# Down projection of the last 64 tokens by fetched table rows, with all up projections first

## The reference, cut to what matters

```python
top_v, top_i = lax.top_k(sc, PEER_TOPK)
...
ids = jnp.take_along_axis(cand_id, best_j, axis=-1)
gates = jax.nn.softmax(best_v, axis=-1)
def block(args):
    xb, ib, gb = args
    ub = jnp.take(u_tab, ib, axis=0)
    a = jnp.einsum('td,ted->te', xb, ub, preferred_element_type=jnp.float32)
    w = gb * jax.nn.gelu(a, approximate=False)
    vb = jnp.take(v_tab, ib, axis=0)
    return jnp.einsum('te,ted->td', w.astype(vb.dtype), vb)
```

## Time and profile before

| | us |
|---|---|
| median of three runs (lowest to highest) | 1292.38 (1290.53 to 1292.54) |
| span of the profiled execution, first to last instruction | 1288.8 |
| PE busy in the span | 1253.4 |
| DVE busy | 980.7 |
| ACT busy | 756.8 |
| POOL busy | 385.8 |

### The profile page before, as it was taken

One profiled execution on the slowest core, in us unless ns is written; L12 is line 12 of the kernel. 1 busy time (PEld: TensorE's weight loads), 2 busy tenths in 40 slices (PEclk: granted clock), 3 DMA queues, 4 the chain that ended last, 5 costly groups with the idle time before them and its releaser, 6 DMA issues.

```text
span 1288.8 us, 26239 instructions
## 1 busy us (share of the span) xinstructions
PE 1253.4 (97%) x8596; PEld 1136.5 (88%) x8596; DVE 980.7 (76%) x1851; ACT 756.8 (59%) x1293; POOL 385.8 (30%) x254
## 2 busy tenths in 40 slices
PE   7999999999999989999999999999999999999997
PEld 7999999898999979999999888888888888888885
DVE  6999988997987767997999765656666666666666
ACT  6434454565766655558999645455555555555554
POOL 1189812225160147788888200000000000000000
PEclk9999999999999999999999999999999999999999
DMA  9978876453776245554443565556665556655662
GB/s 374 336 243 258 263 252 224 162 169 111 246 236 210 92 157 177 168 182 146 129 139 122 163 192 184 193 182 227 210 192 184 184 189 195 183 185 185 195 187 74
DMA packets 69344, 248.15 MB, mean 193 GB/s; under 512 B 7968, under 2 KB 8352, under 8 KB 68512
## 3 DMA queue, kind: packets, MB, share of 16 engines
q1 hardware_dynamic: 59920, 213.04, 51.1%
...
HBM read 244.66 MB, written 2.62 MB: 192 GB/s over the span
## 4 chain that ended last, share of the span: by engine, by line
PE 60%; DVE 8%; ACT 6%; issue 3%; POOL 2%; DMA 0%; DVEq 0%; POOLq 0%; ACTq 0%
PE ps L2525 27%; PE ps L1952 11%; PE ps L2536 10%; PE ps L2538 5%; DVE O L1655 2%; ACT WH L506 2%; DVE O L1646 2%; PE ps L2123 1%; DVE A L1632 1%; ACT A L917 1%; DVE WL L1035 1%; ACT O2b L911 1%; POOL tmp L1891 1%; PE ps L2142 1%; ACT O2b L909 1%
## 5 line engine op out<-in xcount | busy, mean ns | idle before, releaser
L1035 DVE TENSOR_TENSOR WL<-raw,WH 128x1024 fp32r<-128x1024 f32 x320 | 407.1, 1278 | 84.4 <-ACT WH L506 81.1
L506 ACT ACTIVATE WH<-raw 128x1024 fp32r<-128x1024 f32 x392 | 409.8, 1052 | 51.8 <-PE ps L2538 19.6
L1952 PE MATMUL ps<-X,WH 128*128 128x256 f32 x1888 | 349.6, 286 | 2.0 <-DVE WL L1035 1.8
L1952 PEld LDWEIGHTS ps<-X,WH 128*128 128x128 f32 x1888 | 293.4, 192 | 3.1 <-DVE WL L1035 2.4
L1952 PE MATMUL ps<-X,WL 128*128 128x256 f32 x944 | 266.9, 283 | 0.0
L2536 PE MATMUL ps<-X,WH 128*128 128x512 f32 x576 | 205.6, 397 | 0.0
L2525 PE MATMUL ps<-WH,wvL 128*128 128x512 f32 x496 | 195.5, 394 | 0.0
L2525 PE MATMUL ps<-WL,wvH 128*128 128x512 f32 x496 | 195.3, 394 | 0.0
L2525 PE MATMUL ps<-WH,wvH 128*128 128x512 f32 x496 | 195.3, 394 | 0.0
L1918 POOL TENSOR_TENSOR WL<-raw,WH 128x1024 fp32r<-128x1024 f32 x72 | 173.5, 2412 | 59.0 <-ACT WH L506 58.9
L1952 PEld LDWEIGHTS ps<-X,WL 128*128 128x128 f32 x944 | 180.5, 191 | 0.0
...
## 6 DMA issues: line engine op xcount, KB each, us to landing
raw<-stream SPq DMA_DIRECT2D x392, 512.0 KB, 4.2
...
```

The source lines that it names most:

```text
L506: act.activation(WH[:, slot, :], raw[:, slot, :], ACT.Copy).then_inc(h_done, 1)
L1035: dve.tensor_tensor(WL[:, slot, :], raw[:, slot, :], WH[:, slot, :].bitcast(F32), ALU.subtract).then_inc(l_done, 1)
L1952: mm = pe.matmul(out_ap, a(kc), b(kc), start=(first and kc == 0 and i == 0), stop=(last and kc == KC - 1 and i == 2))
```

## The change

The last 64 tokens (OWN) leave the dense down projection.

- **Gates** are built for 192 tokens only: 24 rounds, not 32. So 48 columns have their up before or in a round, and 80 come later.
- **All ups come first**: 80 `up_tile`s in a row, with the same matmuls as before. Their results stay in A, plain gelu for the last 64 tokens, gated for the others.
- **128 downs follow**, of 10 matmuls of 512 columns. Tokens 0 to 127 take three products as before. Tokens 128 to 191 take two: their high and low parts lie interleaved in one stationary operand of 128 columns (`wv`, [P, 2, T, 2]), by WH and by WL. The interleaved halves are added at the end by a matmul with a folding matrix. `wv` is written with a step of 8 bytes.
- **Picking the own scores**, between down steps 2 and 18: for each of 16 groups of 4 tokens, PE spreads the tokens' indices (4 fp16 matmuls of 128 columns), DVE compares (128x512), PE multiplies the one-hot by the tokens' scores (4 fp32 matmuls of 128 columns, whose moving operand steps 1 KiB through A) and DVE picks (4 operations of 128x128).
- **Fetching**: POOL issues 64 indirect DMAs, each of 128 table rows of 4 KB (512 KB: two of the 128 list entries of each of the 64 tokens) into one of three buffers, and DVE multiplies each by a weight per partition and adds it to a sum in PSUM (`own_add`, 128x1024), spread over down steps 22 to 120.
- **POOL makes every third low part** of the down chunks (at steps 0, 3, 6, ..., 123: 42 of 125). Since `l_done` counts in order, each maker waits for the other's.
- The end has four more fp32 matmuls of 512 columns (the fold), and the two halves of tokens change places.

```diff
-EARLY = TOP + T // 8
+OWN = 64
+TD = T - OWN
+ROUNDS = TD // 8
+HOT = TOP + ROUNDS
+EARLY = NK - 2
 C_U = C_WQ + 2 * PH
-C_V1 = C_U + EARLY
-C_UV = C_V1 + EARLY
-LATE = NK - EARLY
-NCHUNK = C_UV + 2 * LATE
-assert C_WQ % RING == 2 and EARLY % RING == 0 and C_UV % RING == 2
+C_D = C_U + NK
+NCHUNK = C_D + NK
+LATE = NK - HOT
+V_ROW = (C_U + EARLY) * P
+assert C_WQ % RING == 2 and (C_U + EARLY) % RING == 0 and LATE % 4 == 0
...
+GROUPS = OWN // 4
+FIRST_PICK = 2
+FIRST_ADD = FIRST_PICK + GROUPS + 4
+ADD_SPAN = NK - 6 - FIRST_ADD
+POOL_EVERY = 3
...
-        wvH = sb("wvH", [P, 2, T], F32R)
-        wvL = sb("wvL", [P, 2, T], F32R)
+        wv = sb("wv", [P, 2, T, 2], F32R)
...
+        def adds_at(j):
+
+            return [k for k in range(OWN) if FIRST_ADD + k * ADD_SPAN // OWN == j]
...
+            def w_high(j):
+                if j >= 2 and j < NK - 1:
+                    act.wait_ge(chunk_done, C_D + j - 1)
+                act.activation(wv_of(j)[:, :, 0], A[:, j, 0:TD], ACT.Copy).then_inc(wh_ready, 1)
...
+            def up_step(i, g=None):
+                tm = tmp[i % 2]
+                act.wait_ge(chunk_done, up(C_U + HOT + i + 1, g, 4))
                 if g is not None or i >= 2:
-                    act.wait_ge(wl_ready, up(EARLY + i - 1, g, 2))
-                act.activation(tmp[i % 2][:, :], ps[:, i % 2, T:2 * T], ACT.Copy).then_inc(half_ready, 1)
-                act.wait_ge(pre_ready, up(i + 1, g, 2))
-                act.activation(tmp[i % 2][:, :], tmp[i % 2][:, :], ACT.Gelu).then_inc(gelu_ready, 1)
-
-            def w_high(i, g=None):
-                act.wait_ge(w_ready, up(i + 1, g, 2))
-                if i == LATE - 1:
-                    act.activation(lastH[:, :], tmp[2 + i % 2][:, :], ACT.Copy).then_inc(wh_ready, 1)
...
+            for j in range(NK):
+                if C_D + 3 + j < NCHUNK:
+                    hi(C_D + 3 + j)
+                if j + 2 < NK:
+                    if j + 2 == HOT:
+                        act.wait_ge(w_ready, LATE)
+                    w_high(j + 2)
+                if j == FIRST_ADD - 2:
...
+            def w_low(j):
+                dve.wait_ge(wh_ready, j + 1)
+                if j >= 2 and j < NK - 1:
+                    dve.wait_ge(chunk_done, C_D + j - 1)
+                dve.tensor_tensor(wv_of(j)[:, :, 1], A[:, j, 0:TD], wv_of(j)[:, :, 0].bitcast(F32),
+                                  ALU.subtract).then_inc(wl_ready, 1)
...
+            def own_compare(q):
+                dve.wait_ge(own_spread, q + 1)
+                if q >= 2:
+                    dve.wait_ge(own_mm, q - 1)
+                dve.tensor_scalar(own_hot[:, q % 2, :, :].rearrange("p t e -> p (t e)"), ps[:, q % 2, :],
+                                  own_part[:, :], None, ALU.is_equal).then_inc(own_hot_ready, 1)
+
+            def own_pick(q):
+
+                dve.wait_ge(own_mm, q + 1)
+                if q >= 1:
+                    dve.wait_ge(own_picked, q)
+                for t in range(4 * q, 4 * q + 4):
+                    pick = dve.scalar_tensor_tensor(out=own_dump[:, t % 4, :], in0=iota, scalar=tmp[2][:, TD + t:TD + t + 1],
+                                                    in1=ps[:, 2 + q % 2, t % 4 * P:t % 4 * P + P], op0=ALU.is_equal,
+                                                    op1=ALU.mult, accum_out=own_act[:, t:t + 1])
+                pick.then_inc(own_picked, 1)
+
...
+            def own_add(k):
+                dve.wait_ge(fetch_in[k % 3], 16 * (k // 3 + 1))
+                if k == 0:
+                    dve.wait_ge(own_w_ready, 2)
+                    dve.tensor_scalar(sums, fetched[0][:, :], own_w[:, 0:1], None, ALU.mult).then_inc(own_added, 1)
                     return
+                dve.wait_ge(own_added, k)
+                dve.scalar_tensor_tensor(out=sums, in0=fetched[k % 3][:, :], scalar=own_w[:, k:k + 1], in1=sums,
+                                         op0=ALU.mult, op1=ALU.add).then_inc(own_added, 1)
+            for j in range(NK):
+                c = C_D + 3 + j
+                if c < NCHUNK and not pool_makes(j):
+                    if j >= 1 and pool_makes(j - 1):
+                        dve.wait_ge(l_done, c)
+                    lo(c)
+                if j + 2 < NK:
+                    w_low(j + 2)
+                q = j - FIRST_PICK
+                if 0 <= q < GROUPS:
+                    own_compare(q)
+                if 1 <= q <= GROUPS:
+                    own_pick(q - 1)
+                if q == GROUPS:
+                    dve.wait_ge(own_picked, GROUPS)
+                    dve.tensor_tensor(own_dump[:, 0, :].rearrange("p (a t) -> p a t", a=2),
+                                      own_act[:, :].unsqueeze(1).broadcast_to([P, 2, OWN]),
+                                      own_gate[:, :].unsqueeze(1).broadcast_to([P, 2, OWN]), ALU.mult).then_inc(own_gated, 1)
+                for k in adds_at(j):
+                    own_add(k)
...
+            def fetch(k):
+                if k >= 3:
+                    pool.wait_ge(own_added, k - 2)
+                pool.indirect_dma_start(fetched[k % 3][:, :], None, stream.rearrange("c p n -> (c p) n"),
+                                        bass.IndirectOffsetOnAxis(ap=own_row[:, k:k + 1], axis=0)
+                                        ).then_inc(fetch_in[k % 3], 16)
+            pool.wait_ge(row_in, 32)
+            pool.wait_ge(chunk_done, C_D)
+            for j in range(NK):
+                c = C_D + 3 + j
+                if c < NCHUNK and pool_makes(j):
+                    pool.wait_ge(l_done, c)
+                    pool_low(c)
+                if j == 0:
+                    for k in range(3):
+                        fetch(k)
+                for k in adds_at(j):
+                    if k + 3 < OWN:
+                        fetch(k + 3)
...
+            def part(j, t, h):
+                slot, w = (C_D + j) % RING, wv_of(j)
+                pe.wait_ge(l_done, C_D + j + 1)
+                pe.wait_ge(wl_ready, j + 1)
+                hs = slice(h * 512, (h + 1) * 512)
+                if t == 1:
+                    both = w[:, P:TD, :].rearrange("p t x -> p (t x)")
+                    products = ((both, WH), (both, WL))
+                else:
+                    products = ((w[:, 0:P, 0], WH), (w[:, 0:P, 0], WL), (w[:, 0:P, 1], WH))
+                for i, (a, b) in enumerate(products):
+                    mm = pe.matmul(ps[:, 4 + 2 * t + h, :], a, b[:, slot, hs], start=(j == 0 and i == 0),
+                                   stop=(j == NK - 1 and i == len(products) - 1), skip_group_check=True)
+                return mm
+            def own_spread_out(q):
+                if q >= 2:
+                    pe.wait_ge(own_hot_ready, q - 1)
+                elif q == 0:
+                    pe.wait_ge(pre_ready, LATE)
+                for t in range(4 * q, 4 * q + 4):
+                    mm = pe.matmul(ps[:, q % 2, t % 4 * P:t % 4 * P + P],
+                                   ident_h[:, P - OWN + t:P - OWN + t + 1].broadcast_to([P, P]), own_i1[:, :],
+                                   start=True, stop=True)
+                mm.then_inc(own_spread, 1)
+            def own_values(q):
+                pe.wait_ge(own_hot_ready, q + 1)
+                if q == 0:
+                    pe.wait_ge(gelu_ready, NK)
+                if q >= 2:
+                    pe.wait_ge(own_picked, q - 1)
+                for t in range(4 * q, 4 * q + 4):
+                    mm = pe.matmul(ps[:, 2 + q % 2, t % 4 * P:t % 4 * P + P], own_hot[:, q % 2, t % 4, :],
+                                   A[:, :, TD + t], start=True, stop=True)
+                mm.then_inc(own_mm, 1)
             pe.wait_ge(gm_ready, ROUNDS)
             pe.wait_ge(gate_out, ROUNDS)
-            fours(pe, EARLY, lambda j, g=None: down(j, C_V1 + j, g, per=4, first=(g is None and j == 0),
...
+            for j in range(NK - 3):
+                q = j - FIRST_PICK
+                if 0 <= q < GROUPS:
+                    own_spread_out(q)
+                if 1 <= q <= GROUPS:
+                    own_values(q - 1)
+                if j == FIRST_ADD - 1:
+                    pe.wait_ge(own_gated, 1)
+                    pe.transpose(ps[:, 0, 0:P], own_dump[:, 0, :], ident)\
+                        .then_inc(own_turned, 1)
+                for t in (1, 0):
+                    for h in range(2):
+                        mm = part(j, t, h)
+                mm.then_inc(chunk_done, 1)
...
+            pe.wait_ge(own_sum_ready, 1)
+            pe.wait_ge(fold_ready, 4)
             for h in range(2):
-                for j in turned:
-                    mm = last_down(j, 1, h)
-                mm.then_inc(token_done, 1)
+                pe.matmul(ps[:, h, :], fold[:, OWN:3 * OWN], own_sum[:, h * 512:(h + 1) * 512], start=True, stop=False,
+                          skip_group_check=True)
+            for j in range(NK - 3, NK):
+                mm = part(j, 0, 0)
+            mm.then_inc(token_done, 1)
```

(6 more changed lines are left out.)

338 lines of the change are left out of this document (143 added, 195 removed).

## The result

The changed kernel takes 1346.4 us (median of four runs, 1344.6 to 1348.8), the kernel before 1291.5 in the same comparison (1289.2 to 1292.5). The ratio is 1.043, with a 95% interval of 1.0415 to 1.0449: slower by 55 us. The prediction was slower, 1304, with 1336 as the upper end. The sign was right, the size lay outside the range by 10 us.

The account below looks back on a forecast made before the run. PE, busy 97% of the span, was taken as the bound. Terms without waits -53.9 us, picking's wait +23.4 and adds +42.1 gave +11.6; 1288.8 + 11.6 + 3.6 = 1304 us, with an 8-in-10 range of 1270 to 1336.

Parts of the forecast that it names:

- Rounds, ups, fewer matmuls: PE: eight rounds gone -33.0 us, their ups later +22.2, two of twelve matmuls fewer in 128 downs -59.1.
- The 8-byte step of `wv`: PE's weight loads in the downs: taken at nothing, since a weight load leaves room.
- The wait that picking adds: Picking steps: PE waits for DVE's compare, queued behind a low part, 1.46 us in each of 16 steps, +23.4.
- two fp32 products hold PE for 0.36 us, 0.18 each, +11.5: Picking on PE: 64 fp32 products at 0.18 us each, +11.5 us.
- fp32 products at 0.4 us or more: Sign listed as showing the forecast wrong: fp32 products taking this long, against 0.18 us forecast.
- the four products at the end: Kernel's end on PE: four fp32 products of 512 columns, 0.72 us each with PE warm, +2.9 us.
- The adds and POOL's low parts: Steps 22 to 123: order and shut-out between POOL and DVE make 277.7 us against PE's 235.6, +42.1.
- the groups with one add: Steps 22 to 123: three-step groups with a single add, 4 times, at PE's own 6.93 us.
- The shut-out: Adds stage: POOL's pass and a DVE operation with two SBUF inputs block each other; a low part took 1.56 us, not 1.23.
- DMA as the bound: Rival, steps 22 to 123: scattered rows take half as long again, 333 us, kernel 1359 us; chance 0.05.
- the step's rival: Picking: the 1 KiB step slows fp32 products to 0.50 us each, +20, kernel 1324 us; chance 0.14.
- the fetch's: Rival, adds stage: a fetch costs POOL 2.41 us, 20 groups grow by 1.37, +27, kernel 1331 us; chance 0.10.

Follow-up runs that it names:

- e2: Changed kernel with the picking's fp32 products reading 128 neighbouring columns of A instead of columns 1 KiB apart (picked values wrong): 1320.0 us.
- e5: Changed kernel with DVE's compare ahead of the weights' low part and the picking's products over neighbouring columns (picked values wrong): 1298.5 us.
- e6: Changed kernel with each fetch that reuses an add's buffer issued one step later in POOL's queue: 1324.4 us.
- e4: Changed kernel with indirect DMAs from the fourth fetch on bringing 256 bytes a row instead of 4 KiB: 1343.6 us.
- e8: Changed kernel with compare ahead of low part, ACT copying picking columns into a neighbouring-column buffer, and POOL's low parts only up to step 18: 1258.1 us.
- e9: e8 with indirect DMAs from the fourth fetch on bringing 256 bytes a row instead of 4 KiB: 1246.9 us.

## Why the prediction was right or wrong

- **Rounds, ups, fewer matmuls: right.** Ups at 2.75 us against 2.77, all of them done at 910 us, DVE and ACT hidden. The 8-byte step of `wv` costs nothing: its weight loads have a median of 193 to 195 ns, where those of a down had a mean of 188 before, and its matmuls start every 0.231 us, as before.
- **The wait that picking adds: right.** +23.4 forecast; e2 against e5 gives 21.4 in 15 steps, 1.43 each against 1.46. A pick takes 0.42 us with the read of its sum, not 0.3, and is hidden all the same.
- **The term that failed: "two fp32 products hold PE for 0.36 us, 0.18 each, +11.5".** The rate was taken from products that read neighbouring columns; the moving operand here steps 1 KiB. They take 0.41 us each, +26 and not +11.5, so about 15 us of the miss. Of the 0.23 us that a product took too much, 0.18 is the step (e2); 0.05 stays over neighbouring columns. This stood among the rivals, at 0.50 us and +20, with a chance of 0.14, and "fp32 products at 0.4 us or more" was one of the prediction's own signs of being wrong. The rival should have been the value taken: ACT's 1.94 ns an element against 1.03 when it writes with the same step was the one row of this case on such a step, while the earlier trace rows has none. The Trainium skill (Advanced Engine Details and Errata, "SBUF Cachelines") says that reads need at least two hits in a line of 16 bytes to run at full speed. The runs agree: reads with 8 bytes of step, two to a line, cost nothing, and with 1 KiB a product takes 0.41 us against 0.23.
- **A term the prediction put at nothing: what the wait and the slow products do together.** It used the clock only for the four products at the end. In the picking the clock fell to 1.2 GHz for 7 to 9 of the matmuls in eight of fifteen steps, some 8 x 0.20 = 1.6 us each time, 12.9 us in all by the table of e5. A step at 2.4 GHz took 5.84, which is the plain sum 3.57 + 1.43 + 4 x 0.18 and 0.1. The four products' 13.8 us over forecast (60 x 0.23) and these 12.9 are the 28.5 us by which the picking missed, but for 1.8. The prediction priced the wait and the step apart, and nothing for the two at once. TensorE: Matmul & The Clock Gate ("HAM oscillation — how this bites in real kernels") of the Trainium skill tells of a kernel whose clock drops at every one of its waits for data, which were longer than those here. The traces agree only in part: waits of 1.28 us came with a drop in the changed kernel and with none in e2, so what ran around the wait decided.
- **The adds and POOL's low parts: right in mechanism, 42.1 forecast and 52.8 measured.** By kind of three steps: adds at 1 and 2 took 9.06 us (8.9 forecast), at 0 and 1 8.29 (8.1), at 0 and 2 8.00 (7.9). The term that was off most is the groups with one add, taken at PE's own 6.93: three of the four took 8.85 and the fourth 7.67, 6.5 of the 11 us. With the fetch one place later (e6) these three take 7.6, so most of it is the order of POOL's queue. The fetch costs POOL 1.45 us in the mean where 1.04 was taken, but the mean is of two kinds, 0.94 and 1.68 us, and the one on the path ahead of the low part in the lines above is the short one. The shut-out is as the earlier trace rows had it, and longer: 2.65 us for a `w_low`.
- **DMA as the bound: not in this kernel, as the chance of 0.05 had it.** e4 gives 3 us. DMA's limit comes at 2.45 us a step (e8, e9), under the 2.84 that the turns set.
- **The range.** The forecast with the step's rival is 1324, with the fetch's too 1351. Each stood alone in its own case, and the upper end, 1336, had room for one of them and not for both. That 1351 lies near the measured 1346 is chance: the fetch never cost the 2.41 us of that rival, and the 12.9 us of the clock were in no rival. Rivals that don't exclude each other have to be summed for the end of a range.
